# A hybrid attention and state-space decode layer on one core: one pair of state-space heads per attention head, and an output projection that opens with the attention rows of four tiles

## The chip, the cores and the metric

The kernel runs on one core of a Trainium2 chip. The metric is the device time of one execution in microseconds, lower is better. TensorE (PE) does the matmuls, VectorE (DVE) and ScalarE (ACT) the elementwise work, GpSimd (POOL) helps, and SyncE (SP) issues every DMA in one queue of instructions.

## The reference, cut to what matters

One layer mixes latent attention (8 heads) and a Mamba-2 state-space mixer (16 heads in 2 groups) over 512 prompt tokens, and takes one step for 8 decoding sequences. Both branches are gated and go through one output projection with a norm and a residual.

```python
p = softmax(q_lat @ ckv.T + q_rope @ k_rope.T)          # per attention head, causal
o_attn = (p @ ckv) @ w_uv * silu(z_attn)
y_diag = einsum('bcgls,bgjcls,bcsgjp->bclgjp', cb, exp(segsum(a)), xdt)
y_off  = einsum('bclgn,bcgjpn,bgjcl->bclgjp', cc, states, exp(a_cum))
h = exp(da)[..., None, None] * h + outer(x * dt, b)     # decode step: new state
y_s = h . c                                             # and its dot with c
g = (y + d * xs) * silu(z_ssm)
y_ssm = rmsnorm(g, per group of 512 columns)
out = x + rmsnorm(concat(o_attn, y_ssm) @ w_out)
```

## The kernel before, in words

Everything is transposed: 128 partitions hold a slice of the features, the free axis holds 512 prompt and 8 decode tokens (520 columns, worked on in two halves of 260). Each projection matmul is done as three (low part of the weights, low part of the data, high parts), so ACT rounds each weight tile of 128x1024 to `w_hi` (`hi(i)`, L553), DVE makes `w_lo` from it (`lo(i)`, L880), and then PE can use it.

The work comes in stages, each written out by hand for every engine, with semaphores between the engines and no planner:

- input projection with the paged attention of the decode tokens in its gaps, items 0 to 39 of `ITEMS` (0 to 312 us in the trace);
- states of the state-space mixer and values of attention (to about 346 us);
- the attention loop over 8 heads with the rest of the mixer in its gaps (346 to 481 us). Here one pass of the loop is called a slot: in slot s PE does the scores of head s+1 (L1758 to L1760, four blocks through three PSUM banks), the transposes of the probabilities of head s (`probs_t`, L1768), the keys of head s+2 (`keys`, L1747) and the products with the values (`outs`, L1776). DVE takes each block's maximum (`mask_max`) and the reciprocal of its sum (`inverse_sum`), ACT the exponential (`exps`, L762) and the copy of the transposes (`copy_pt`, L770), POOL scales the probabilities (`norm`), DVE gates the result (`gated`, L1224);
- the output projection (from 481.5 us), items 40 to 71: eight output tiles m for each half h, each from two weight tiles: attention rows (k2 = 0) and state-space rows (k2 = 1), eight steps k of three matmuls each. `out_square` squares the finished tile, DVE copies it out with a scale (L1352).

In the gaps of the attention loop lies the mixer:

- Eight pairs of state-space heads. A pair needs two decay tiles from ACT (`decays`, L723 and L726, each loaded by SP with `load_acb` into a ring of six), a multiplication each on DVE (`head`, L1157), PE's matmuls (`y_pair`, L1723 and L1726), and three operations on DVE that take the result out (`y_pair`, L1163 to L1165). POOL then gates it (`gate`, L1426), ACT squares it, POOL adds the squares. Before, slots 0 to 3 hold two pairs each and slots 4 to 7 none.
- After four pairs, `group_sum` totals the squares of a group on PE, `group_root` takes the root on ACT (L595), `inverse` the reciprocal on DVE (L914), `group_scale` applies it to four tiles (L1239), `ssm_high` (ACT, L780) and `ssm_low` (DVE, L1233) split each tile into the parts that the output projection reads.
- Sixteen half states of the decode step ("quads"): `state_decay` on ACT (L733), four updates on DVE (L1175) and the `dots` (L1182, L1183). Before, `SLOT_QUADS` puts ten into slots 1 to 7 and `ITEM_QUADS` six into the output projection, one to every second item. `sample_gate` and `sample_norm` follow once all are done; they release the state-space rows of the second half.

Before, the first half of the output projection starts each tile with its state-space rows; the second half starts with the attention rows. SP issues the states 2 to 7 after the last pair, then stores states 0 and 1, then loads the tiles 40 and 41, and after the last product of attention tiles 42 and 43, the residual `xres_g` and tile 44.

Of the kernel before, what the change touches and what calls it, by code (L numbers as in the profile page):

```python
# [11 lines left out]
F = mybir.dt.float32  # L12
R = mybir.dt.float32r
I32 = mybir.dt.int32
ALU = mybir.AluOpType
# [27 lines left out]
         + [("out", h, m, k, 1 - k if h == 0 else k) for h in range(2) for m in range(8) for k in range(2)])  # L43
# [7 lines left out]
NIN_UNITS = UNIT0[NIN]  # L51

# [18 lines left out]
INV0 = [0, 2, 4, 6, 7, 8]  # L71
# [7 lines left out]
for _h in range(H):  # L79
    RING += [("t", _h, 0), ("t", _h, 1)] + ([("k", _h + 2)] if _h + 2 < H else []) + [("t", _h, 2), ("t", _h, 3)]  # L80
    RING += [("sum", _h // 2 - 1)] if _h in (3, 5) else []
# [3 lines left out]
SLOT_QUADS = {1: {3: 0}, 2: {3: 1}, 3: {3: 2}, 4: {3: 3}, 5: {3: 4, 4: 5}, 6: {3: 6, 4: 7}, 7: {1: 8, 3: 9}}  # L85
ITEM_QUADS = {NIN + 2 * n: 10 + n for n in range(6)}
FIRST_NEEDS = {(NIN, 0): 13, (NIN, 6): 14, (NIN, 7): 15, (NIN + 1, 7): 16}
GROUP_SCALE = {4: (0, 1), 5: (2, 3), 6: (4, 5, 6, 7)}
SSM_HIGH = {5: (0, 1), 6: (2, 3), 7: (4, 5, 6, 7)}
SSM_LOW = {5: (0, 1), 6: (2, 3), 7: (4, 5), 8: (6, 7)}  # L90
# [16 lines left out]
def build(nc, a):  # L107
# [7 lines left out]
    def sem(name):  # L115
# [8 lines left out]
             + [at(f"hring{b}", [P, 8, NS], F, A_ + 4096 * (b - 2)) for b in range(2, NB)])  # L124
# [132 lines left out]
    a_mask = sem("mask_rounded")  # L257
# [20 lines left out]
    v_mlo, v_zs, a_zh = sem("mix_lo_done"), sem("sample_gated_copied"), sem("sample_gated_high")  # L278
# [3 lines left out]
    g_acm, g_n, g_gate, g_order = sem("acum_masked"), sem("probs_normed"), sem("ssm_gated"), sem("pool_order")  # L282
# [24 lines left out]

    def quads(s, b):

        return [SLOT_QUADS[s][b]] if b in SLOT_QUADS.get(s, ()) else []  # L310
# [29 lines left out]
    def _(sp):  # L340
        def load_item(i):
# [11 lines left out]
            elif it[0] == "qb":  # L353
                sp.dma_start(w_raw[s][:, 0:768], a["w_qb"][it[1]]).then_inc(s_wl[s], 16)
            else:
                sp.dma_start(w_raw[s], a["w_out"][it[2], it[4]]).then_inc(s_wl[s], 16)
# [120 lines left out]
        load_bcs(1)  # L477
        for t in range(5):
# [1481 lines left out]
```

## Time and profile before

| | us |
|---|---|
| median of 3 runs (592.9 to 593.53) | 593.33 |
| the profiled execution | 591.05 |
| its span | 589.3 |
| PE busy in the span | 531.9 (90%) |
| DVE busy | 384.9 (65%) |
| ACT busy | 290.6 (49%) |
| POOL busy | 77.7 (13%) |
| granted TensorE clock, mean | 0.967 |

The span is what the profiler saw; the execution is 1.75 us longer. A busy share is a mean over stages that have different limits, so the stages have to be read one by one. The clock is the share of full speed that was granted: 1.00 is the upper of its two levels (2.4 GHz), 0.50 the lower (1.2 GHz), values between are stretches with some of both.

### The profile page before, as it was taken

The numbers are of one execution on the slowest core, as the hardware profiler recorded it, in microseconds if no ns is written. First come the engines' busy times: TensorE is split into PE (matmuls) and PEld (weight loads), VectorE is DVE, ScalarE is ACT, GpSimd is POOL, SyncE is SP. The second block draws the span as 40 slices with busy tenths as digits, with TensorE's granted clock in tenths as the row PEclk, the third lists the DMA queues.
The fourth block names the chain that finished last, engine by engine and source line by source line (L and its number), as shares of the span: only waits on it lengthen the run. The fifth ranks groups of instructions, "written<-read, shape, count | busy, mean of one in ns | idle before, by whom it ended". The sixth has DMA issues, their size and how long they took to land.

```text
span 589.3 us, 12342 instructions
## 1 busy us (share of the span) xinstructions
PE 531.9 (90%) x4726; PEld 449.1 (76%) x4726; DVE 384.9 (65%) x735; ACT 290.6 (49%) x624; POOL 77.7 (13%) x102
## 2 busy tenths in 40 slices
PE   4999998999999999999998999898787639999992
PEld 4899997998888888888885456566543339999992
DVE  5674987766555677445334753767677898795675
ACT  7333232143565554552614754877858645645320
POOL 2110000000000000000002412433431000210520
PEclk9999999999999999999999999888989959999997
DMA  8233032296889877788753342432470083669552
GB/s 333 108 143 97 30 97 86 71 315 222 255 268 283 265 256 250 239 309 289 246 191 97 93 133 82 110 81 60 148 256 19 6 303 115 223 202 367 188 157 72
DMA packets 55692, 104.12 MB, mean 177 GB/s; under 512 B 7193, under 2 KB 25986, under 8 KB 55378
## 3 DMA queue, kind: packets, MB, share of 16 engines
q1 hardware_dynamic: 55634, 103.33, 53.7%
q8 instruction: 38, 0.62, 0.4%
q14 instruction: 20, 0.16, 0.1%
HBM read 95.68 MB, written 7.73 MB: 175 GB/s over the span
## 4 chain that ended last, share of the span: by engine, by line
PE 76%; DVE 14%; ACT 6%; issue 3%; DMA 1%; POOL 0%; DVEq 0%; SPq 0%; ACTq 0%
PE pm L1488 18%; PE pm L1490 16%; PE pm L1489 16%; PE px L1571 4%; PE px L1587 3%; PE px L1760 3%; PE px L1758 3%; PE pm L1709 2%; ACT dec L723 1%; PE pm L1747 1%; DVE hring L1175 1%; PE px L1700 1%; PE px L1723 1%; DVE w_lo L880 1%; DVE xbc L1239 1%
## 5 line engine op out<-in xcount | busy, mean ns | idle before, releaser
L1488 PE MATMUL pm<-xw_hi,w_lo 128*128 128x260 f32 x544 | 162.3, 298 | 9.4 <-DVE w_lo L1007 8.3
L1489 PE MATMUL pm<-xw_lo,w_hi 128*128 128x260 f32 x544 | 154.4, 284 | 0.0
L1490 PE MATMUL pm<-xw_hi,w_hi 128*128 128x260 f32 x544 | 154.2, 283 | 0.0
L1488 PEld LDWEIGHTS pm<-xw_hi,w_lo 128*128 128x128 f32 x544 | 103.0, 189 | 24.6 <-issue 11.9
L553 ACT ACTIVATE w_hi<-w_raw 128x1024 fp32r<-128x1024 f32 (+1 forms) x70 | 72.0, 1035 | 83.0 <-PE pm L1490 76.7
L880 DVE TENSOR_TENSOR w_lo<-w_raw,w_hi 128x1024 fp32r<-128x1024 f32 (+1 forms) x70 | 85.9, 1236 | 29.0 <-ACT w_hi L553 29.0
L1489 PEld LDWEIGHTS pm<-xw_lo,w_hi 128*128 128x128 f32 x544 | 103.1, 190 | 0.2
L1490 PEld LDWEIGHTS pm<-xw_hi,w_hi 128*128 128x128 f32 x544 | 103.1, 189 | 0.0
L1488 PE MATMUL pm<-mix_hi,w_lo 128*128 128x260 f32 x256 | 73.7, 288 | 11.8 <-DVE mixlo_s L1233 11.3
L1490 PE MATMUL pm<-mix_hi,w_hi 128*128 128x260 f32 x256 | 73.2, 286 | 0.0
L1488 PEld LDWEIGHTS pm<-mix_hi,w_lo 128*128 128x128 f32 x256 | 49.2, 192 | 12.4 <-issue 12.1
L1490 PEld LDWEIGHTS pm<-mix_hi,w_hi 128*128 128x128 f32 x256 | 49.0, 191 | 0.0
L1489 PE MATMUL pm<-mixlo_s,w_hi 128*128 128x260 f32 x128 | 37.0, 289 | 0.0
L1489 PE MATMUL pm<-mixlo_a,w_hi 128*128 128x260 f32 x128 | 36.1, 282 | 0.0
L1210 DVE TENSOR_REDUCE nmx<-px 128x1 f32<-128x128 f32 (+3 forms) x32 | 15.3, 484 | 25.8 <-PE px L1760 25.7
L1758 PE MATMUL px<-kn,q 128*128 128x128 f32 (+3 forms) x64 | 25.4, 481 | 7.4 <-ACT pr L762 7.3
L625 ACT ACTIVATE alpha<-nmh 128x1 f32<-128x1 f32 x32 | 9.4, 295 | 45.7 <-DVE nmh L960 45.6
L971 DVE SCALAR_TENSOR_TENSOR ckbc<-ckbc,alpha,px 128x256 f32<-128x256 f32 x32 | 15.4, 481 | 24.4 <-PE px L1587 23.8
L1420 POOL TENSOR_SCALAR pr<-pr,rsum 128x128 f32<-128x128 f32 (+3 forms) x32 | 20.4, 643 | 71.9 <-DVE rsum L1216 71.0
L619 ACT ACTIVATE ptb<-px 128x128 f32<-128x128 f32 x32 | 8.7, 273 | 42.2 <-PE px L1580 42.2
L1776 PE MATMUL pm<-pt,v 128*128 128x512 f32 (+3 forms) x64 | 22.4, 450 | 7.3 <-ACT pt L770 7.3
L947 DVE SCALAR_TENSOR_TENSOR u<-xbc,cols,u 128x511 f32<-128x511 f32 (+2 forms) x36 | 26.4, 748 | 0.8
(273 smaller groups left out, 1048.7 us busy)
## 6 DMA issues: line engine op xcount, KB each, us to landing
page<-in_cache SPq DMA_DIRECT2D x128, 288.0 KB, 3.6
w_raw<-in_w_in SPq DMA_DIRECT2D x34, 512.0 KB, 5.0
w_raw<-in_w_out SPq DMA_DIRECT2D x32, 512.0 KB, 4.7
dec<-ac_dram SPq DMA_DIRECT2D x16, 256.0 KB, 9.1
hring<-in_ssm_state SPq DMA_DIRECT2D x8, 512.0 KB, 6.5
o_ssms<-hring SPq DMA_DIRECT2D x8, 512.0 KB, 7.0
w_raw<-in_w_qb SPq DMA_DIRECT2D x6, 384.0 KB, 3.0
xraw<-in_xT SPq DMA_DIRECT2D x4, 520.0 KB, 6.4
```

What stands on the lines that cost most here:

```text
L553: act.activation(w_hi[s][:, 0:n], w_raw[s][:, 0:n], ACT.Copy).then_inc(a_whi, 1)
L880: dve.tensor_tensor(w_lo[s][:, 0:n], w_raw[s][:, 0:n], w_hi[s][:, 0:n].bitcast(F), ALU.subtract)\
L947: last = dve.scalar_tensor_tensor(b[:, s:NT], xbc[:, t, 0:NT - s], col(C_CW + 4 * t + 3 - s), b[:, s:NT], ALU.mult, ALU.add)
L1420: pool.tensor_scalar(x, x, rsum[:, k:k + 1], 0.0, ALU.mult, ALU.add).then_inc(g_n, 1)
L1488: pe.matmul(out, wl, xh, start=start, stop=False)
L1489: pe.matmul(out, wh, xl, start=False, stop=False)
L1490: return pe.matmul(out, wh, xh, start=False, stop=stop)
L1571: last = pe.matmul(px[32 * j:32 * j + 32, n % 2, lo_:lo_ + n_], w, x, start=op == 0, stop=op == 3)
L1587: last = pe.matmul(px[32 * j:32 * j + 32, 3, 0:KVR], ptb[:, n % 2, 32 * j:32 * j + 32], page[:, n % 4, j, 0:KVR], start=True, stop=True)
L1758: pe.matmul(px[:, n % 3, 0:w], q[:, h, P * b:P * b + P], kn[:, h % 2, 0:w], start=True, stop=False)
L1760: pe.matmul(px[:, n % 3, 0:w], q[:, 8 + h // 2, P * b:P * b + P], krz[h % 2][:, 0:w], start=False, stop=True)\
L1776: pe.matmul(pm[:, 3, P * kb:NT], v[:, kb, VH * h:VH * h + VH], pt[:, toff(kb):toff(kb) + NT - P * kb], start=kb == 0, stop=kb == 3).then_i ...
```

## The change

- `PAIRS`: slot 0 does two pairs of state-space heads, slots 1 to 6 one each (pair s+1). Their decays, heads, gates and squares follow the same rhythm.
- `HEAD_QUAD`: six half states in slots 1 to 6. `ITEM_QUADS`: ten in the output projection, to items 43, 44, 46, 47, 49, 50, 51, 52, 54 and 55.
- The engines' orders inside a slot are rewritten. PE puts the two first transposes before the fourth block of scores. `state_update` is taken out of `dots`.
- The group factor is made on ACT as a logarithm and an exponential (`group_log`, `group_factor`) in place of root on ACT and reciprocal on DVE. Group 0 is totalled in slot 6, group 1 after item 40.
- The output projection does, in each half, the attention rows of tiles 0 to 3, then their state-space rows, then tiles 4 to 7 one by one, attention rows first.
- The finished tile is copied out by ACT right after its square, no longer by DVE.
- SP: state 2 is loaded in the loop (it has a new place), states 0 and 1 are stored before the last pair, tiles 40 and 41 are issued right after the last pair and states 3 to 7 behind them.

```diff
-         + [("out", h, m, k, 1 - k if h == 0 else k) for h in range(2) for m in range(8) for k in range(2)])
+         + [("out", h, m, k) for h in range(2) for m0 in (0, 4, 5, 6, 7) for k in range(2)
+            for m in (range(4) if m0 == 0 else (m0,))])
+PAIRS = {0: (0, 1), **{s: (s + 1,) for s in range(1, 7)}}
+HEAD_QUAD = {s: s - 1 for s in range(1, 7)}
+ITEM_QUADS = {NIN + k: 6 + n for n, k in enumerate((3, 4, 6, 7, 9, 10, 11, 12, 14, 15))}
...
# SP, after the loads of the loop
+        load_bcs(2)
         load_ea(7)
+        store_state(0)
+        load_bcs(3)
+        store_state(1)
         sp.wait_ge(p_y, 8)
+        load_item(NIN)
+        sp.wait_ge(s_hs0, 32)
+        load_item(NIN + 1)
         for b in range(3, NB):
             load_state(b)
+        load_bcs(4)
         sp.wait_ge(s_out, 48)
         load_item(NIN + 2)
         load_item(NIN + 3)
         sp.dma_start(xres_g, a["xT"][:, 0:7]).then_inc(s_xr, 16)
...
# ACT, slot s
+            exps(s + 1, 0)
+            exps(s + 1, 1)
+            if s == 6:
+                group_log(0, r_pre)
+            copy_pt(s, 0)
+            exps(s + 1, 2)
+            if s == 6:
+                group_factor(0, r_pre)
+            copy_pt(s, 1)
+            if s:
+                mix_high(s - 1)
+                exp_ea(s + 1)
...
+            if 1 <= s <= 5:
+                decays(2 * s + 4)
+            exps(s + 1, 3)
+            if s:
+                gated_square(s)
+            if s + 2 < H:
+                copy_k(s + 2)
+            copy_pt(s, 2)
+            copy_pt(s, 3)
+            if 1 <= s <= 5:
+                decays(2 * s + 5)
+            if s + 1 in HEAD_QUAD:
+                state_decay(HEAD_QUAD[s + 1])
# ACT, output projection
         for i in range(NIN, len(ITEMS)):
             if i + 3 < len(ITEMS):
                 hi(i + 3)
+            if i == NIN:
+                group_log(1, sqs)
+                group_factor(1, sqs)
+            if i in (NIN + 1, NIN + 2):
+                for t in range(2):
+                    ssm_high(4 + 2 * (i - NIN - 1) + t)
...
# DVE, slot s
+            mask_max(s + 1, 0)
+            mask_max(s + 1, 1)
+            if 2 <= s <= 6:
+                head(2 * s + 3)
+            inverse_sum(s + 1, 0)
+            mask_max(s + 1, 2)
+            inverse_sum(s + 1, 1)
+            if n is not None:
+                state_update(n)
+            mask_max(s + 1, 3)
             if s:
                 mix_low(s - 1)
...
+            inverse_sum(s + 1, 2)
+            y_pair(PAIRS[s][0])
+            if 1 <= s <= 5:
+                head(2 * s + 4)
+            inverse_sum(s + 1, 3)
+            if n is not None:
+                dots(n)
+            if s == 6:
+                for t in range(4):
+                    group_scale(t)
             gated(s)
# DVE, between the loop and item 40
+        lo(NIN)
+        mix_low(H - 2)
+        ssm_low(0)
+        ssm_low(1)
+        gated(H - 1)
+        lo(NIN + 1)
         mix_low(H - 1)
+        ssm_low(2)
+        ssm_low(3)
# DVE, output projection
             if i + 3 < len(ITEMS):
                 lo(i + 3)
+            if i in (NIN + 2, NIN + 3):
+                ssm_low(2 * (i - NIN))
+                ssm_low(2 * (i - NIN) + 1)
+            if i in (NIN + 1, NIN + 2):
+                group_scale(2 * (i - NIN) + 2)
+                group_scale(2 * (i - NIN) + 3)
             for n in item_quads(i - 1):
+                state_update(n)
                 dots(n)
-            if i == NIN + NOUT - 4:
+            if i == NIN + NOUT + 1:
                 sample_gate()
...
# PE, slot h
             if h + 1 < H:
-                scores(h + 1)
+                scores(h + 1, range(3))
+            if h == 6:
+                group_sum(0)
             probs_t(h, 0)
             probs_t(h, 1)
-            if h < 4:
-                y_pair(2 * h)
+            if h + 1 < H:
+                scores(h + 1, (3,))
+            if h in PAIRS:
+                y_pair(PAIRS[h][0])
# PE, output projection
             for k in range(8):
-                if (i, k) in FIRST_NEEDS:
-                    pe.wait_ge(v_mlo, FIRST_NEEDS[i, k])
+                if n == 0:
+                    pe.wait_ge((v_mla, v_mls)[k2], k + 1)
...
-            if i == NIN + NOUT - 1:
+            if i == NIN:
+                group_sum(1)
+            if i == NIN + NOUT + 1:
                 pe.wait_ge(v_gs, 1)
```

## Rows read from the trace of the kernel before

**Rows 1.** Windows: busy us (and instructions) of each engine, granted clock, DMA, by slot.

```profile
core 0: us, PE busy (x) PEld busy (x) DVE busy (x) ACT busy (x) POOL busy (x), PEclk, DMA share, GB/s
366.09:384.26 18.17, 15.40 (x88) 10.82 (x87) 11.40 (x24) 14.86 (x42) 6.71 (x7) 0.88 0.44 112
384.26:403.76 19.50, 16.64 (x87) 11.86 (x87) 12.69 (x26) 15.08 (x43) 7.94 (x8) 0.85 0.32 80
...
421.44:432.00 10.56, 10.20 (x44) 6.19 (x43) 8.54 (x18) 7.89 (x19) 4.89 (x7) 1.00 0.92 318
...
448.05:462.79 14.74, 10.39 (x39) 6.03 (x38) 11.15 (x27) 11.01 (x25) 1.31 (x3) 0.88 0.07 18
462.79:481.51 18.72, 4.13 (x21) 2.33 (x19) 18.27 (x32) 8.49 (x19) 0.81 (x2) 0.75 0.46 173
481.51:500.00 18.49, 18.49 (x138) 18.49 (x139) 16.09 (x25) 11.89 (x22) 0.75 (x1) 0.88 0.49 161
```

**Rows 2.** Timeline of PE: start, length, line, operation, [idle before, releaser].

```profile
371.72 1.09 PE L1723 MATMUL px<-dec,xdt 128*64 128x128 f32 x16
...
373.51 1.88 PE L1747 MATMUL pm<-ckv,w_uk 128*128 128x512 f32 x4
...
481.51 0.56 PE L1488 MATMUL pm<-mix_hi,w_lo 128*128 128x260 f32 x1 [11.29 <-DVE mixlo_s L1233]
```

**Rows 3.** Timeline of ACT, attention loop.

```profile
376.27 1.26 ACT L723 ACTIVATE dec<-dec,acum 128x128 f32<-128x128 f32 x4
377.57 0.63 ACT L726 ACTIVATE dec<-dec 128x512 f32<-128x512 f32 x1
...
418.62 1.28 ACT L595 ACT_TABLE_LOAD   x1
```

**Rows 4.** Timeline of DVE, attention loop.

```profile
371.67 1.78 DVE L1175 SCALAR_TENSOR_TENSOR hring<-bcs,dxs,hring 128x128 f32<-128x128 f32 x4
...
378.84 0.74 DVE L1163 SCALAR_TENSOR_TENSOR xbc<-xbc,cols,px 128x512 f32<-128x512 f32 x1
...
380.69 0.68 DVE L1224 TENSOR_TENSOR u<-pm,z 128x512 f32<-128x512 f32 x1
...
430.35 3.33 DVE L914 RECIPROCAL r_pre<-r_pre 128x512 f32<-128x512 f32 x1
...
470.56 2.73 DVE L1239 SCALAR_TENSOR_TENSOR xbc<-xbc,cols,sqs 128x512 f32<-128x512 f32 x4
...
481.88 1.28 DVE L1233 TENSOR_TENSOR mixlo_s<-xbc,mix_hi 128x512 fp32r<-128x512 f32 x2
```

**Rows 5.** Timeline of POOL, slot 1.

```profile
371.23 1.28 POOL L1426 TENSOR_TENSOR xbc<-xbc,z 128x512 f32<-128x512 f32 x1
```

**Rows 6.** Timeline of ACT, output projection.

```profile
512.49 0.39 ACT L581 ACTIVATE sq<-pm 128x260 f32<-128x260 f32 x1 [0.46 <-PE pm L1490]
...
515.42 1.06 ACT L553 ACTIVATE w_hi<-w_raw 128x1024 fp32r<-128x1024 f32 x1 [0.43 <-PE pm L1490]
...
518.25 0.39 ACT L581 ACTIVATE sq<-pm 128x260 f32<-128x260 f32 x1 [1.76 <-PE pm L1490]
```

**Rows 7.** Timeline of DVE, output projection.

```profile
506.60 1.23 DVE L880 TENSOR_TENSOR w_lo<-w_raw,w_hi 128x1024 fp32r<-128x1024 f32 x1 [2.69 <-ACT w_hi L553]
...
515.85 1.13 DVE L1175 SCALAR_TENSOR_TENSOR hring<-bcs,dxs,hring 128x128 f32<-128x128 f32 x4
...
518.41 0.48 DVE L1352 TENSOR_SCALAR outp<-pm,cols 128x260 f32<-128x260 f32 x1
...
526.24 0.21 DVE L1188 TENSOR_TENSOR gs<-xbc,cols 128x64 f32<-128x64 f32 x1
...
527.46 1.21 DVE L880 TENSOR_TENSOR w_lo<-w_raw,w_hi 128x1024 fp32r<-128x1024 f32 x1
```

**Rows 8.** SP's issues of output weight tiles, and their time to landing, 468 to 475 us.

```profile
470.25 0.82 SPq L356 DMA_DIRECT2D w_raw<-in_w_out  x2
...
472.77 0.97 SPq L356 DMA_DIRECT2D w_raw<-in_w_out  x1
...
DMA to landing us min/median/max: 7.4/8.3/11.8
```

More of the change, by code:

```diff
@@ L51 @@
 NIN_UNITS = UNIT0[NIN]
+HALVES = [sum(it[0] == "out" and it[3] == 0 for it in ITEMS[:i + 1]) for i in range(len(ITEMS))]
 NSTEP = 2 * NPAGE
@@ L477, in _ @@
         load_bcs(1)
+        uk = {1: 4, 2: 5, 3: 6, 4: 7}
         for t in range(5):
@@ L802, in _ @@
         copy_k(1)
-        for s in range(-1, H):
-            h = s + 1
-            for b in range(4):
-                if h < H:
-                    exps(h, b)
-                if s >= 0 and b >= 2:
-                    copy_pt(s, b - 2)
-                if b == 1 and 1 <= s <= 4:
-                    gated_square(2 * s - 2)
-            if s < 0:
-                act.wait_ge(v_zs, 1)
-                act.activation(mix_hi[:, 0:H, NT:TT], zs, ACT.Copy).then_inc(a_zh, 1)
-                decays(5)
-                continue
+        for b in range(4):
+            exps(0, b)
@@ L845, in _ @@
+        gated_square(H - 1)
+        ssm_high(0)
+        ssm_high(1)
+        hi(NIN + 1)
         mix_high(H - 1)
+        ssm_high(2)
+        ssm_high(3)
         hi(NIN + 2)
@@ L1269, in _ @@
         dve.wait_ge(v_os, 1)
-        for s in range(-1, H):
-            h = s + 1
-            for b in range(4):
-                if h < H:
-                    mask_max(h, b)
-                if b == 0 and 2 <= s <= 3:
-                    head(4 * s)
-                    head(4 * s + 1)
-                if b == 1 and 1 <= s <= 4:
-                    y_pair(2 * s - 1)
-                for n in quads(s, b):
-                    dots(n)
-                if h < H and b:
-                    inverse_sum(h, b - 1)
-            if h < H:
-                inverse_sum(h, 3)
-            if s < 0:
-                continue
-            if s in (4, 6):
-                inverse(s // 2 + 1, (r_pre, sqs)[s // 2 - 2])
+        for b in range(4):
+            mask_max(0, b)
+            if b:
+                inverse_sum(0, b - 1)
+        inverse_sum(0, 3)
+        for s in range(H - 1):
+            n = HEAD_QUAD.get(s)
+            mask_max(s + 1, 0)
[8 more added lines that the diff above has]
+            mask_max(s + 1, 3)
             if s:
@@ L1439, in add_square @@
                 .then_inc(g_sqg, 1)
-        for s in range(-1, H):
-            h = s + 1
-            for b in range(4):
-                if h < H:
-                    norm(h, b)
-                if b == 1 and 1 <= s <= 4:
-                    gate(2 * s - 1)
-            if 1 <= s <= 4:
-                add_square(2 * s - 2)
-            if 0 <= s <= 3:
-                gate(2 * s)
-            if 1 <= s <= 4:
-                add_square(2 * s - 1)
+        for b in range(4):
+            norm(0, b)
+        for s in range(H - 1):
+            norm(s + 1, 0)
+            norm(s + 1, 1)
+            if s == 6:
+                add_square(5)
+            if s:
+                gate(s)
+            norm(s + 1, 2)
+            norm(s + 1, 3)
+            if s == 0:
+                gate(0)
+            elif s != 5:
+                add_square(s)
+        gate(H - 1)
+        add_square(H - 1)
         def out_add(h, j):
@@ L1753, in scores @@
                 pe.wait_ge(a_mask, 2)
-            for b in range(4):
+            for b in blocks:
                 n, w = 4 * h + b, P * (b + 1)
@@ L1806, in _ @@
         pe.wait_ge(v_st, 2 * NCH)
-        scores(0)
+        scores(0, range(4))
         pe.wait_ge(v_os, 1)
```

207 lines of the change are left out of this document (85 added, 122 removed).

## The prediction

> **What bounds the kernel now.** I read the slices of the page first: PE is busy nine tenths everywhere but in the attention loop and its end. The windows by slot [rows 1] size that. Slots 1 to 5 last from 366.09 to 448.05, 82.0 us, 16.4 each; slot 4, the only one with neither a pair nor a reciprocal, takes 10.56 and has PE at 10.20 busy. A pair adds 1.79 on PE (371.72 to 373.51) [rows 2], so two pairs explain 13.8 of the 18.17 and 19.50 in slots 1 and 2. The rest is waiting, and the clock: it is granted at 0.88 and 0.85 there. ACT is the fullest helper, 15.08 of 19.50, because two pairs cost it four decay tiles at 1.9 each [rows 3]. In slot 5 and slot 7 a reciprocal of 3.33 sits in DVE's queue [rows 4]. After the last product of attention PE stands still for 11.29 until 481.51 and waits for a low part that DVE makes [rows 2]; DVE is 18.27 of 18.72 busy there [rows 1]: it is behind, and it is what sets the start of the output projection. From there on PE runs solid: two items between two squares, 512.49 to 518.25, so 2.88 each [rows 6], 92.2 for the 32, and 2.2 lost to the clock at the start ((1 - 0.88) x 18.49) [rows 1].
>
> **The attention loop.** One pair per slot. PE's work in a slot is 10.20 + 1.79 = 12.0. ACT falls from 15.08 by two decay tiles to about 11.2, DVE from 12.69 by one evacuation of a pair (378.84 to 380.69, 1.85) [rows 4] and the removed reciprocals to some 10.8. Both fit under 12.0. Walking the slot in the new order, each hand-over has slack: the fourth scores need only the first exponential, made 1 us earlier; the transposes at the slot's start need POOL's last scaling, finished some 3 us before; a decay tile is loaded a slot or more before its use, and SP's new waits inside the loop (dots of quad 1, v_y of pair 5) stand in front of loads for two slots later. I take 12.1. No idle of PE means no fall of the clock either. Slots 1 to 5: 5 x 12.1 = 60.5 against 82.0, **-21.5**. Slot 0 I leave as it is.
>
> A bound from the other side: no gain, 16.4 a slot.
>
> **Slots 6 and 7.** Before, 448.05 to 470.22 (481.51 - 11.29), 22.2. Now the last pair is in slot 6, and DVE must take it out (1.85), do the dots (515.85 to 518.41 is 2.56 with the 1.13 of the updates, so 1.43) [rows 7] and four scales (2.73) [rows 4] before it gates head 6 (0.6), for which the products of head 7 wait. PE finishes the pair 9.2 into the slot (12.0 less the products); 9.2 + 6.6 + hand-overs 0.6 = 16.4, and the products of head 7, most of the 4.13 in [rows 1], end at 19.6. **-2.6**. The removed reciprocal would have been on this path. The logarithm for group 0 is in front of the second transpose: an exponential's table has to be left and fetched again.
>
> A switch of function cost ACT 1.28 in front of the root [rows 3]; I charge the same on the way to the logarithm and again to the exponential, since before has neither a logarithm nor a row that excludes either load: 0 or 1.28 each. By the Trainium skill (ScalarE: Activation LUTs, Table sets) one shipped set holds exponential and logarithm, which would make it one load in place of two. The trace agrees with the 1.28 and cannot show the rest.
>
> **From the last product to the end of the fifth item.** Before: 11.29 + 5 x 2.88 + 2.2 = 27.9. Now PE starts almost at once, on attention rows. But item 44 is the first with state-space rows, and its steps 4 to 7 need tiles 4 to 7, whose factor is made only after item 40. Let Z be the end of the last product. SP may issue item 42 only at Z (+0.4), then 43, the residual, 44. Before, 42 left at 470.25 and 44, issued at 472.77, landed 11.8 later [rows 8], 14.3 after 42. So 44 lands at Z + 14.7. Five state loads moved to just before can only make it later; I take nothing for them, as they have 10 us to drain. Then ACT and DVE go in turns, since the code puts each `hi` and `lo` before the tile work of its item: hi(44) 1.06 [rows 6], lo(44) 1.2 [rows 7], two scales 1.4, `ssm_high` 0.6, hi(45) 1.06, lo(45) 1.2, two low parts 1.3 [rows 4], two scales 1.4, `ssm_high` 0.6, hi(46) 1.06, lo(46) 1.2, two low parts 1.3, the last step 0.4: 13.8. Item 44 ends at Z + 28.5 and not at Z + 14.4. **+0.6** against before: the 11.29 of idle is not removed but moved into item 44. Its cover is only the three items 41 to 43, 8.6.
>
> **The rest of the output projection.** The same 27 items. DVE loses 16 evacuations of 0.48 [rows 7], which ACT takes at about the length of a square, 0.39, beside matmuls; it is half idle there (11.89 of 18.49) [rows 1]. At the very end the copy lies behind the square and beside PE's total, so nothing; without that cover 0.4. But DVE gets ten quads in 13 items where it had six in 11. A quad costs it 2.56, a `lo` 1.2: 3.8 in an item of 2.88. From item 43's end at Z + 28.1 it needs 14 x 1.2 + 10 x 2.56 + 1.2 for the gate (526.24 to 527.46) = 43.6, so `sample_gate` is done at Z + 71.7. PE waits for it behind item 57, which it has finished at Z + 28.5 + 13 x 2.88 = Z + 65.9. **+5.8** of standstill, where before had 0.5 at most. The weights themselves stay ahead. Both standstills are followed by half clock, 2.2 each as at 481.51: **+4.4**. The tail is the same work.
>
> **Sum.** -21.5 - 2.6 + 0.6 + 5.8 + 4.4 = -13.3. Against the profiled execution: 591.05 - 13.3 = 577.75; the median of the runs lies 2.28 above that execution, so 580.0.
>
> **Rivals.**
> - *Tiles 42 to 44 land sooner.* They had to share with the residual; with other neighbours a landing of 7.4 instead of 11.8 [rows 8] ends item 44 some 6 earlier, 574. For it: the state loads are gone from the queue by then. Against: the same three issues in the same order took what they took. Chance 0.2.
> - *The gate's wait does not bite*, because DVE regains in items 40 to 43 what I charge it later: 5.8 + 2.2 less, 572. Against: it has no gap in my walk. Chance 0.12.
> - *Fewer table loads.* Two of 1.28 leave the path, one in slot 6 and one ahead of item 44 if the load isn't what it waits for: 577.5. This is what the rule on table sets above would give. Chance 0.12.
> - *The slots don't shrink (the slower one).* Place: the hand-overs DVE, ACT, PE in slots 1 to 5. The mechanism is in the trace: four updates of a quad took 1.78 from 371.67 on, with POOL's gate running from 371.23 [rows 4, 5], and 1.13 elsewhere [rows 7]; now the updates stand in front of the fourth maximum, beside POOL's gate in every slot, and a late fourth maximum delays exponential, scaling and transposes, PE idles, and the clock falls as in slots 1 and 2. At 14.0 per slot the time is 589.5; from 14.8 the gain of 13.3 is used up; at the 16.4 of before it is 601.5. Against: some 3 us of slack in each step. Chance 0.18, of it 0.08 beyond 14.8 and 0.03 at it. The Trainium skill (GPSIMD Engine Reference, Key points) has GpSimd and VectorE share their SBUF interfaces when VectorE reads two SBUF inputs, which is this update; the trace agrees (1.78 beside POOL, 1.13 alone).
>
> **How the numbers follow.** My forecast 0.38, the rivals 0.2, 0.12, 0.12 and 0.18. A change under 0.2% can't be told from none here. Faster 0.89, same 0.03, slower 0.08. The range: down to two of the better cases together (580 - 6 - 8 = 566) and a little for slot 0, 564; up to 14.0 per slot, 589.
>
> **What would show it.** In the profile after: windows of 12 us per slot with PE near full and the clock at 1.00 (wrong: PE waiting for ACT's `pr` or `pt`, 14 and more). DVE's scales and the gate of head 6 ahead of the products of head 7. PE's largest wait inside item 44, released by `mixlo_s`, some 14 long in all, and hi(44) waiting for its load. DVE above 95% busy from item 44 to 57, then a wait of about 6 of PE on `gsum`. If the first is missing, -21.5 was wrong; if the second or third, the time is better by 6 to 14.

## The result, and the profile after

The changed kernel takes **579.9 us** (median of 4 runs, 578.05 to 581.02) against 593.43 (592.9 to 593.91) for the kernel before: a ratio of 0.9761, 95% interval 0.9733 to 0.979. It is faster by 13.5 us. The profiled execution took 580.6, with a span of 578.7.

One thing first, as every comparison below hangs on it. The input stage, which the change doesn't touch, doesn't end at the same time in every execution. The first scores of attention start here:

```profile
346.37 0.39 PE L1758 MATMUL px<-kn,q 128*128 128x128 f32 x2
...
348.97 0.39 PE L1779 MATMUL px<-kn,q 128*128 128x128 f32 x2
```

These are PE's timelines of the kernel before and of the one after. In the twelve experiments the same instruction starts at 346.47 to 346.71 seven times and at 348.85 to 348.95 five times. So I measure stages within one execution, and spans "from the scores": 242.9 before (589.3 - 346.37), 229.7 after. That is -13.2; the forecast's sum was -13.3.

The windows of the kernel after, columns as in [rows 1]: slots 0, 1 and 5 of the attention loop; slots 6 and 7 together; from the last product to the end of item 44; from there to the gate's matmul; the rest up to the last items.

```profile
353.73:367.99 14.26, 14.20 (x87) 9.15 (x86) 6.26 (x17) 8.15 (x25) 4.64 (x7) 1.00 0.44 148
367.99:379.82 11.83, 11.83 (x66) 7.61 (x65) 10.47 (x22) 8.52 (x24) 4.41 (x6) 1.00 0.71 158
...
415.31:427.14 11.83, 11.83 (x67) 7.61 (x65) 9.97 (x21) 10.45 (x31) 3.96 (x5) 1.00 0.43 126
427.14:450.79 23.65, 17.18 (x83) 10.66 (x81) 17.51 (x27) 15.19 (x35) 8.08 (x8) 0.86 0.45 166
450.79:477.80 27.01, 17.94 (x126) 16.38 (x126) 17.79 (x22) 18.30 (x29) 1.30 (x1) 0.88 0.69 239
477.80:522.95 45.15, 39.15 (x313) 38.94 (x312) 41.86 (x78) 29.50 (x62) 5.53 (x6) 0.92 0.72 220
522.95:568.30 45.35, 45.31 (x346) 44.46 (x346) 23.04 (x26) 17.67 (x30) 12.00 (x12) 0.93 0.49 146
```

The first number is the window, the second PE's busy time. In slots 1 to 5 they are equal, at full clock (slots 2 to 4 are like 1 and 5): where [rows 1] had 18.17 and 19.50, PE now never waits. From 427.14 on it does again, and the view of waits for PE names the places (line, what is awaited; total, times, longest):

```profile
PE px L1881 <- DVE gsum L1207: 6.0, 1, 6.0
PE pm L1509 <- DVE mixlo_s L1248: 5.9, 2, 3.8
PE pm L1797 <- DVE u L1239: 4.8, 1, 4.8
PE pm L1509 <- DVE mixlo_a L1243: 2.1, 1, 2.1
PE pm L1509 <- ACT sqs L592: 1.1, 1, 1.1
```

The first four are DVE's. Slots 6 and 7 (behind the wait on `u`), on DVE, POOL and PE:

```profile
430.82 3.36 DVE L1190 SCALAR_TENSOR_TENSOR hring<-bcs,dxs,hring 128x128 f32<-128x128 f32 x4
435.02 0.69 DVE L1225 TENSOR_REDUCE nmx<-px 128x1 f32<-128x512 f32 x1 [0.83 <-PE px L1781]
...
440.57 4.62 DVE L1254 SCALAR_TENSOR_TENSOR xbc<-xbc,cols,r_pre 128x512 f32<-128x512 f32 x4
445.12 0.68 DVE L1239 TENSOR_TENSOR u<-pm,z 128x512 f32<-128x512 f32 x1
```
```profile
439.23 1.19 POOL L1435 TENSOR_SCALAR pr<-pr,rsum 128x512 f32<-128x512 f32 x1 [1.31 <-DVE rsum L1231]
440.39 1.26 POOL L1453 TENSOR_TENSOR gacc<-gacc,sq 128x512 f32<-128x512 f32 x1
441.61 1.71 POOL L1441 TENSOR_TENSOR xbc<-xbc,z 128x512 f32<-128x512 f32 x1
```
```profile
445.95 2.05 PE L1797 MATMUL pm<-pt,v 128*128 128x512 f32 x2 [4.82 <-DVE u L1239]
...
450.79 0.37 PE L1509 MATMUL pm<-mix_hi,w_lo 128*128 128x260 f32 x1
```

The four scales take 4.62 where [rows 4] had 2.73; POOL is busy during 2.7 us of them. The product that then starts takes 2.05; at 436.70, ahead of the wait, the same form took 1.02. The next view has the items up to 44, with ACT and DVE in turns.

```profile
459.00 1.28 ACT L592 ACT_TABLE_LOAD   x1
460.30 0.69 ACT L592 ACTIVATE sqs<-pm,epsc 128x512 f32<-128x512 f32 x1
461.00 1.28 ACT L597 ACT_TABLE_LOAD   x1
462.30 0.63 ACT L597 ACTIVATE sqs<-sqs 128x512 f32<-128x512 f32 x1
463.50 1.06 ACT L549 ACTIVATE w_hi<-w_raw 128x1024 fp32r<-128x1024 f32 x1 [0.57 <-DMA w_raw<-in_w_out]
466.52 1.29 ACT L781 ACTIVATE mix_hi<-xbc 128x512 fp32r<-128x512 f32 x2 [1.96 <-DVE xbc L1254]
467.72 1.04 ACT L549 ACTIVATE w_hi<-w_raw 128x1024 fp32r<-128x1024 f32 x1
471.92 1.29 ACT L781 ACTIVATE mix_hi<-xbc 128x512 fp32r<-128x512 f32 x2 [3.16 <-DVE xbc L1254]
...
477.78 0.39 ACT L577 ACTIVATE sq<-pm 128x260 f32<-128x260 f32 x1 [0.33 <-PE pm L1511]
```
```profile
464.60 1.23 DVE L896 TENSOR_TENSOR w_lo<-w_raw,w_hi 128x1024 fp32r<-128x1024 f32 x1 [4.35 <-ACT w_hi L549]
465.74 1.41 DVE L1254 SCALAR_TENSOR_TENSOR xbc<-xbc,cols,sqs 128x512 f32<-128x512 f32 x2
468.79 1.23 DVE L896 TENSOR_TENSOR w_lo<-w_raw,w_hi 128x1024 fp32r<-128x1024 f32 x1 [1.65 <-ACT w_hi L549]
469.94 1.29 DVE L1248 TENSOR_TENSOR mixlo_s<-xbc,mix_hi 128x512 fp32r<-128x512 f32 x2
...
475.33 1.28 DVE L1248 TENSOR_TENSOR mixlo_s<-xbc,mix_hi 128x512 fp32r<-128x512 f32 x2
```

Each engine is idle while the other works: 4.35 and 1.65 on DVE, 1.96 and 3.16 on ACT. The logarithm has a load ahead of it and the exponential another, 1.28 each.

### The profile page after: what moved, and what is told of

Its sections match the earlier page's. It is cut to its first block, busy times and chain, and to the rows that moved or that the text cites. A ratio compares the mean times of both kernels' runs of the same rounds, so it can differ in the third digit from the quotient of the medians.

```text
span 578.7 us, 12372 instructions
## 1 busy us (share of the span) xinstructions
PE 531.7 (92%) x4726; PEld 450.4 (78%) x4726; DVE 379.3 (66%) x717; ACT 297.3 (51%) x642; POOL 78.9 (14%) x102
## 4 chain that ended last, share of the span: by engine, by line
PE 75%; DVE 14%; ACT 4%; issue 3%; DMA 3%; SPq 0%; DVEq 0%; ACTq 0%
PE pm L1509 16%; PE pm L1511 14%; PE pm L1510 14%; PE px L1592 4%; PE pm L1797 3%; PE px L1608 3%; PE px L1781 3%; DVE w_lo L896 3%; PE px L1779 3%; PE pm L1768 2%; PE pm L1730 2%; DMA w_raw<-in_w_out 2%; DVE hring L1190 2%; ACT w_hi L549 2%; PE pm L1789 1%
## 5 line engine op out<-in xcount | busy, mean ns | idle before, releaser
L1509 PEld LDWEIGHTS pm<-xw_hi,w_lo 128*128 128x128 f32 x544 | 103.5, 190 | 24.7 <-issue 11.9
L896 DVE TENSOR_TENSOR w_lo<-w_raw,w_hi 128x1024 fp32r<-128x1024 f32 (+1 forms) x70 | 85.2, 1220 | 44.4 <-ACT w_hi L549 44.3
L1509 PE MATMUL pm<-mix_hi,w_lo 128*128 128x260 f32 x256 | 76.0, 297 | 9.1 <-DVE mixlo_s L1248 5.9
L1511 PE MATMUL pm<-mix_hi,w_hi 128*128 128x260 f32 x256 | 74.6, 291 | 0.0
L1509 PEld LDWEIGHTS pm<-mix_hi,w_lo 128*128 128x128 f32 x256 | 50.7, 198 | 10.4 <-DVE mixlo_s L1248 6.6
L1511 PEld LDWEIGHTS pm<-mix_hi,w_hi 128*128 128x128 f32 x256 | 50.6, 198 | 0.0
L1797 PE MATMUL pm<-pt,v 128*128 128x512 f32 (+3 forms) x64 | 24.4, 482 | 4.8 <-DVE u L1239 4.8
L1190 DVE SCALAR_TENSOR_TENSOR hring<-bcs,dxs,hring 128x128 f32<-128x128 f32 x64 | 27.8, 494 | 0.0
L1425 POOL TENSOR_TENSOR xdte<-xdt,toend 128x512 f32<-128x512 f32 x8 | 10.2, 1278 | 121.2 <-DVE xdt L1152 121.2
```

Source lines behind the costliest of these rows:

```text
L896: dve.tensor_tensor(w_lo[s][:, 0:n], w_raw[s][:, 0:n], w_hi[s][:, 0:n].bitcast(F), ALU.subtract)\
L1190: dve.scalar_tensor_tensor(hring[b][:, t, :], bcs[b % 2][:, g, :], dxs[:, 0, t, b:b + 1], hring[b][:, t, :], ALU.mult, ALU.add).then_inc(v ...
L1509: pe.matmul(out, wl, xh, start=start, stop=False)
L1511: return pe.matmul(out, wh, xh, start=False, stop=stop)
L1797: pe.matmul(pm[:, 3, P * kb:NT], v[:, kb, VH * h:VH * h + VH], pt[:, toff(kb):toff(kb) + NT - P * kb], start=kb == 0, stop=kb == 3).then_i ...
```

## The experiments

Each is the changed kernel with the edit shown. "From the scores" is the span of the profiled execution less the start of the first scores in it; it comes from one execution, the median from four (six in experiment 9). The two measures differ by up to about 4 us in what they make of an edit, so both are given.

| | experiment | us (range) | ratio to before | from the scores |
|---|---|---|---|---|
| | kernel after | 579.9 (578.05 to 581.02) | 0.9761 | 229.7 |
| 1 | head 6's gate first | 574.02 (573.29 to 575.45) | 0.9693 | 226.5 |
| 2 | item 44's tiles at once | 573.66 (570.17 to 574.45) | 0.967 | 223.3 |
| 3 | 1 and 2 | 568.43 (566.26 to 571.01) | 0.9573 | 217.9 |
| 4 | 2, opens with two tiles | 575.21 (573.78 to 577.37) | 0.9697 | 225.3 |
| 5 | residual later | 576.19 (575.96 to 576.36) | 0.9731 | 227.6 |
| 6 | root and reciprocal | 584.62 (584.0 to 586.94) | 0.9885 | 233.5 |
| 7 | thin half states, loop | 577.07 (576.22 to 578.65) | 0.9725 | 227.7 |
| | thin half states, projection | 571.19 (568.9 to 572.78) | 0.9626 | 220.4 |
| 8 | 3, half states early | 569.82 (569.41 to 571.46) | 0.9592 | 223.1 |
| 9 | 8, residual later, head 7 first | 569.69 (569.28 to 574.33) | 0.9614 | 221.1 |
| 10 | 9, gate's matmul later | 570.35 (569.35 to 572.45) | 0.9612 | 219.3 |
| 11 | 10, one half state ahead of item 40 | 566.09 (565.18 to 569.81) | 0.9544 | 216.2 |

My theory: three walls stand behind the loop, all DVE's: `u` ahead of the last products, the rows of item 44, the gate's sums. The rivals, one for each: the fourth maximum late through the state update; the landing of item 44's weights; a stall that PE would have wherever it asks.

**1. Head 6's gate ahead of the four scales.**

```
+            gated(s)
             if s == 6:
                 for t in range(4):
                     group_scale(t)
-            gated(s)
```

> The changed kernel (579.9) with one move: in slot 6 DVE gates head 6 before the four scales of group 0. Theory: PE's wait of 4.82 before the products of head 7 is DVE's order and nothing else. The products then start about 4.6 earlier, at full clock (2.7 for them in place of 4.84), and the scales fall into time in which DVE waited (3.76) for ACT's high parts. The end of the last product comes 5 to 7 earlier, but item 44 hangs on item 42's issue at that end, so it comes earlier too: total 573 to 575. Rival: the scales are then late for the low parts and for item 40's last step, and the gain is lost in items 40 to 44: total 578 to 580.

574.02. From the start of slot 6 (424.64) to the first matmul of the output projection is 445.02 - 424.64 = 20.38 instead of 23.65, and the wait on `u` is gone: the last product ends at 442.04, 17.4 into the slot. A new one stands one place on: the scales now delay the low part of item 40's weights. PE:

```profile
445.02 0.59 PE L1509 MATMUL pm<-mix_hi,w_lo 128*128 128x260 f32 x1 [2.98 <-DVE w_lo L896]
```

So 3.3 us are won up to there, and all of the gain is made there (3.2 from the scores): a wait of 4.8 was cured, and one of 3.0 took its place.

**2. The rows of item 44 in one piece.** The four scales, then the four low parts, ahead of the next weight tile's low part; the four high parts together on ACT.

```
+            if i == NIN + 1:
+                for t in range(4, 8):
+                    group_scale(t)
+                for t in range(4, 8):
+                    ssm_low(t)
             if i + 3 < len(ITEMS):
                 lo(i + 3)
-            if i in (NIN + 2, NIN + 3):
...
```

> The changed kernel with one reordering: the four scales, high parts and low parts of tiles 4 to 7 are done in one go, before hi(44) on ACT and lo(44) on DVE, and not in turns with hi and lo of items 44 to 46. Theory: item 44 is late because of the turns. The last low part is ready some 7 earlier, PE's two waits on mixlo_s (2.11 and 3.77) vanish and with them most of the half clock after: item 44 ends 18 to 21 after the last product in place of 26.9, total 571 to 574, if DVE's gate wait of 6.0 behind item 57 stays as it is. Rival one, the loads decide: hi(44) waited for its load anyway, so item 44 ends at most 2 earlier, total 578. Rival two, DVE decides: what item 44 gains comes back as a longer wait behind item 57 (12 in place of 6), total 579.

573.66. The waits on `mixlo_s` are gone; what stays inside item 44 is 2.1 on `w_lo`. From the last product (450.76) to item 44's square is 22.0 instead of 27.0, and the item behind it takes 2.88 instead of 4.58, as PE doesn't come out of a standstill at half clock. The sums' wait is 6.4.

**3. Both.**

> The first two edits together: head 6 of the attention before the gate of the last slot, and item 44's ssm tiles first. By the spans from the start of the attention loop they saved 3.2 and 6.4 us alone. Theory (one cures the wait behind slot 6, the other the wait before item 44, two places): most of both is kept, 7 to 9 us from 579.9, so 571 to 573 us. Rival (both are paid for by the same VectorE backlog that the gate's sums wait for): the wait on gsum grows to 8 to 9 us and 573.5 to 575 us result, no better than the second alone.

568.43, below what I expected. By medians the two saved 5.9 and 6.2 and together 11.5; from the scores 3.2 and 6.4 and together 11.9, which is 2.3 more than the sum, and no run here shows why. They add at least, and the rival of one common backlog falls. The two largest waits of PE in this kernel:

```profile
PE px L1879 <- DVE gsum L1206: 6.4, 1, 6.4
PE pm L1507 <- DVE w_lo L895: 5.1, 2, 3.0
```

**4. Opening with two tiles.** Experiment 2, with the first half of the projection opening on the attention rows of two tiles.

```
+         + [("out", h, m, k) for h in range(2) for m0 in ((0, 2) if h == 0 else (0,)) + (4, 5, 6, 7) for k in range(2)
+            for m in (range(m0, m0 + 4 - 2 * (h == 0)) if m0 < 4 else (m0,))])
```

> The kernel with the pair of ssm tiles of item 44 first, and the first half of the output projection opens with the attention rows of two tiles (as the second item list of the kernel before did with its halves) instead of four; so the Mamba rows are asked for after four items instead of eight. Theory (the four-tile opening is what gives the chain of the Mamba rows time: some 12 us of PE work in four items more): PE meets item 42 with the first state rows about 11 us earlier, of which the rows' chain can't follow; waits on the mixed rows grow by 3 to 5 us, and 577 to 579 us result against 573.7. Rival (DVE's total work until the gate's sums is the bound, and the order of the items only places the wait): the wait on gsum shrinks by what the new waits take, and 573 to 575 us result.

575.21, between the two: 1.6 slower by medians, 2.0 from the scores. PE waits 4.20 on `mixlo_s` instead of 2.1 on `w_lo`, and the sums' wait stays at 6.4. The ranges of the two kernels overlap, but the wait agrees with the difference. So the four-tile opening is worth about 2 us with the rows' chain already shortened; how much it gave with the chain of the changed kernel was not run.

**5. The residual's load four items later.**

```
-        sp.dma_start(xres_g, a["xT"][:, 0:7]).then_inc(s_xr, 16)
...
+            if i == NIN + 8:
+                sp.dma_start(xres_g, a["xT"][:, 0:7]).then_inc(s_xr, 16)
```

> The changed kernel with the residual (1820 KB) issued behind item 47's tile in place of ahead of item 44's. Rival of the prediction (tiles land sooner): item 44's load is what the chain begins with, so item 44 ends 5 to 6 earlier and the total is 574. Theory after the trace: ACT waited only 1.40 for item 43's load and 0.57 for item 44's; between them lie two table loads, logarithm and exponential. So the chain can start at most 2.0 earlier: total 578 to 579.9.

576.19, 3.7 less by medians and 2.1 from the scores, against 0 to 1.9 expected and 5.9 by the rival. Item 44 ends 25.95 after the last product instead of 27.0, and `mixlo_s` is waited for 5.6 instead of 5.9. So the landing is worth 1 us. A further 0.9 is the item behind it at 3.72 instead of 4.58; that varies: 4.76 in experiment 1, 3.53 in experiment 7, after waits of the same 3.8 to 4.2.

**6. Root on ACT and reciprocal on DVE in place of logarithm and exponential.**

```
-            act.activation(dst[:, 0:NT], pm[:, bank(("sum", g)), :], ACT.Ln, bias=epsc, scale=1.0 / NORM_WIDTH[3 + g])\
+            act.activation(dst[:, 0:NT], pm[:, bank(("sum", g)), :], ACT.Sqrt, bias=epsc, scale=1.0 / NORM_WIDTH[3 + g])\
...
+                dve.reciprocal(r[:, 0:NT], r[:, 0:NT]).then_inc(a_gf, 1)
```

> The changed kernel with one part undone: the group factors are made by a root on ACT and a reciprocal on DVE as before, in place of logarithm and exponential on ACT. Theory: DVE gets 3.3 twice, in slot 6 in front of the scales that delay the gate of head 6, and in front of the scales of tiles 4 and 5; ACT loses 0.6 twice and one table load before item 44 (the one back to the exponential). Slot 6: 2.5 to 3.3 later. Item 44: 3.3 less 1.9, 1.4 later. Total 583 to 585. Rival: the reciprocal lies in time in which DVE waits, total 580.

584.62: the logarithm form is worth 4.7 by medians and 3.8 from the scores. DVE between the dots and the gate of head 6:

```profile
440.28 3.34 DVE L1252 RECIPROCAL r_pre<-r_pre 128x512 f32<-128x512 f32 x1
...
443.66 2.74 DVE L1255 SCALAR_TENSOR_TENSOR xbc<-xbc,cols,r_pre 128x512 f32<-128x512 f32 x4
```

The wait on `u` is 6.31, only 1.5 more for a reciprocal of 3.34, because the same four scales, now begun when POOL's gates of this place are over, take 2.74 and not 4.62. The total lies in the forecast range, but not by the parts that were forecast: the start of the output projection is 0.9 later in its slot (expected 2.5 to 3.3), and from there to item 44's square it takes 30.0 instead of 27.0 (expected 1.4 more), with 8.4 of waiting on `mixlo_s` instead of 5.9.

**7. Thin half states.** Two kernels whose state updates and dots work on 16 of 128 state columns (so they leave out 112 columns of the new state and of its output): one in the six half states of slots 1 to 6, one in the ten of the projection.

```
+            c = 16 if n < 6 else NS
...
+                dve.scalar_tensor_tensor(hring[b][:, t, 0:c], bcs[b % 2][:, g, 0:c], dxs[:, 0, t, b:b + 1], hring[b][:, t, 0:c], ALU.mult, ALU.add).then_inc(v_h, 1)
```

> The changed kernel with less work on DVE in the attention loop: the six half states of slots 1 to 6 are updated and dotted in 16 of their 128 state columns only (112 are left out). Theory: slots 1 to 5 are bound by PE, so they stay at 11.83 each to the hundredth, although DVE loses about 2 of its 10 in each. In slot 6 DVE's queue sets the gate of head 6: the dots (1.4) shrink to about 0.4, so PE's wait of 4.82 falls by about 1, total 1 to 2 less, 578 to 579. Rival: the slots hang on DVE and shrink by 0.3 or more each, total 576 or less.

> The changed kernel with less work on DVE in the output projection: the ten half states there are updated and dotted in 16 of 128 state columns only (112 are left out). Theory: DVE saves about 1.9 in each of ten, the sample's gate is ready long before item 57 ends, PE's wait of 6.0 on gsum vanishes with the half clock behind it (2.2), total 571 to 572. Item 44 ends where it did. Rival: the wait is released by something else (the weights of item 60, the load for item 58 for which ACT waited 2.2), then 3 or more of the 6.0 stay: total 575 to 577.

In the loop (577.07, between the 578 expected at least and the rival's 576) they are free: from the scores to slot 6 is 78.16 against 78.17. In slot 6 the update shrinks from 3.36 to 0.80, and the maximum behind it doesn't move, 432.71 - 424.83 = 7.88 into the slot as in the kernel after (435.02 - 427.14):

```profile
428.52 0.80 DVE L1191 SCALAR_TENSOR_TENSOR hring<-bcs,dxs,hring 128x16 f32<-128x16 f32 x4
432.71 0.69 DVE L1227 TENSOR_REDUCE nmx<-px 128x1 f32<-128x512 f32 x1 [3.39 <-PE px L1783]
```

What this kernel still gains lies in the dots ahead of `u` (last product 23.0 into slot 6 instead of 23.65) and in the clock behind item 44. The wait on `u` falls only from 4.8 to 4.6 and not by 1: `u` is ready 0.7 earlier in the slot, and PE asks for it 0.5 earlier. In the projection the same edit gains 8.7 (9.3 from the scores): the sums' wait falls from 6.0 to 0.8, though item 44 waits no less (6.8 on `mixlo_s`, before 5.9). This leaves the work out and moves it nowhere. The window from item 44 to the gate:

```profile
474.90:513.91 39.01, 38.21 (x312) 38.00 (x311) 27.42 (x78) 29.52 (x62) 4.51 (x6) 0.98 0.75 241
```

**8. The ten half states one or two items earlier,** on experiment 3, with the rows of their `bcs` buffer loaded four items earlier.

```
-ITEM_QUADS = {NIN + k: 6 + n for n, k in enumerate((3, 4, 6, 7, 9, 10, 11, 12, 14, 15))}
+ITEM_QUADS = {NIN + k: 6 + n for n, k in enumerate((1, 2, 4, 5, 7, 8, 10, 11, 13, 14))}
...
-        bc_after = {NIN + 13: 5, NIN + 16: 6, NIN + 19: 7}
+        bc_after = {NIN + 9: 5, NIN + 12: 6, NIN + 15: 7}
```

> The changed kernel with the gate of head 6 first, the state-space tiles 4 to 7 in one go, and the ten half states of the output projection moved ahead, to items 41, 42, 44, 45, 47, 48, 50, 51, 53 and 54 (the loads of their rows three to four items earlier). The first two edits gave 5.9 and 6.2 less by themselves; if they add, 568. Theory on the quads: two in three items are 2 x 3.7 + 1.1 = 8.5 of DVE in 8.64 of PE, so DVE keeps up, the last is done at item 55 and the wait on gsum falls from 6.0 to under 1, with the half clock 6 to 8 less: total 560 to 562. Rival: the two early ones delay lo(45) and lo(46) and PE waits there instead, 4 or more: total 564 to 567.

A miss: 569.82, no better than experiment 3 and 5.2 worse from the scores. The wait on the sums was to fall under 1 and is 5.4, and the waits on `w_lo` are 7.2 instead of 5.1. The edit moved a wait into SP's queue. SP after the last product:

```profile
471.99 2.90 SPq L354 DMA_DIRECT2D w_raw<-in_w_out  x3
481.10 0.38 SPq L429 DMA_DIRECT2D bcs<-bc_dram  x1
481.52 0.73 SPq L354 DMA_DIRECT2D w_raw<-in_w_out  x1
```

The load of `bcs` waits for the dots that still use its buffer, from 474.89 to 481.10, and no weight tile goes out in that time. ACT's waits of that stretch, first in this kernel and then in experiment 3:

```profile
ACT w_hi L549 <- DMA w_raw<-in_w_out: 12.2, 5, 4.0
...
ACT w_hi L549 <- DMA w_raw<-in_w_out: 0.7, 1, 0.7
```

DVE then idles 4.4 of 49.9 us (45.51 busy) where it idles 1.6 of 46.1 in experiment 3. So the queue accounts for DVE's idle time, and with it for the wait on the sums that stays; no run takes that wait out of the queue, so this is argued from the trace. It doesn't account for all of the 5.2: 1.1 comes earlier, where ACT waits 2.3 for the tiles of items 42 and 43 and not 1.2, loads that the edit doesn't touch; 2.7 lies between there and the sums, 1.4 behind them. The profiled execution was also the slowest of its four (571.46, the others 569.41 to 570.06).

**9. On 8, the residual later and head 7's rows first.**

```
         lo(NIN)
         mix_low(H - 2)
-        ssm_low(0)
-        ssm_low(1)
         gated(H - 1)
-        lo(NIN + 1)
         mix_low(H - 1)
+        lo(NIN + 1)
+        ssm_low(0)
+        ssm_low(1)
```

> The kernel of the run before it in this list, with two more edits: the residual issued behind item 47's tile, and between the loop and item 40 the gate and low part of head 7 ahead of the low parts of tiles 0 and 1 (ACT likewise makes head 7's high part first). Theory: PE's wait of 2.1 for head 7's low part in item 40 falls to under 1, and item 42's and 44's loads come up to 1.4 earlier: 2 to 3 less, 558 to 560. Rival: item 40 then waits for its own weights, whose low part DVE makes behind the scales, and nothing changes.

That is DVE's order; ACT makes its high parts in the same one. 569.69, the same by medians, 2.0 less from the scores; the sums' wait is 5.6. The wait for head 7's low part, which the edit was to shorten, stood in the kernel after (2.1) but isn't in experiment 8 at all: the gate of head 6 ahead of the scales had already removed it. That reordering had nothing to win.

**10 and 11. The gate's matmul two items on; then one half state ahead of item 40.**

```
-            if i == NIN + NOUT + 1:
+            if i == NIN + NOUT + 3:
                 pe.wait_ge(v_gs, 1)
...
# 11, and no half state at item 41
         ssm_low(2)
         ssm_low(3)
+        state_update(6)
+        dots(6)
```

> The combination of the last run (quads early, residual later, head 7 first) and, besides, the column sums' matmul two items further back on PE (behind item 59 instead of 57), the gate's norm behind item 60 instead of 59, the inverse one item later. Theory (the 6.0 us wait is VectorE's total work between item 41 and item 57, met by PE wherever it asks for the sums): PE goes on with items 58 and 59, about 5.8 us of work, while VectorE finishes; the wait on gsum falls from 5.6 to 0 to 1 us, and 566 to 568 us result against 569.7, less than the whole 5.6 because the norm's chain behind the sums is then met at item 61 or 62 with some 2 to 3 us. Rival (the rest of the gate's chain is as long as the wait): the wait only moves to the first matmul that needs the norm, 569 to 570 us.

> As the kernel with the sums' matmul behind item 59, and one of the output projection's ten half states (a 128 x 512 scale row and its dots, some 2.5 us of VectorE) is done before item 40, in time in which VectorE waits for ScalarE. Theory (VectorE's total work from there to item 57 is the bound): 1 to 2.5 us less than that kernel, 564.5 to 567 us. Rival (this half state delays the w_lo of items 40 to 42, which PE waits for): the waits on w_lo grow by 2 to 3 us and nothing is won, or it is 1 us slower.

In 10 the steps behind the matmul (root, norm, inverse) come one or two items later too. Experiment 10: 570.35, no gain that its median shows, 1.8 from the scores. By its total the rival is nearer than the theory. PE goes through items 58 and 59 at full clock, and the sums aren't waited for. The wait is then met by the matmul that needs the rows made from them; PE in 10:

```profile
515.54 0.29 PE L1880 MATMUL px<-gsum,cm 128*128 128x16 f32 x2
...
518.57 0.36 PE L1508 MATMUL pm<-mix_hi,w_lo 128*128 128x260 f32 x1 [2.73 <-DVE mixlo_s L1219]
```

2.73 for 5.62. Half of what was left of the gain went into waits on `w_lo` (6.7 to 8.1). Experiment 11: 566.09, 4.3 less by medians, 3.1 from the scores. The half state fills idle time of DVE ahead of item 40; PE's waits on `w_lo` grow by only 0.5, and ACT still waits 16.4 for weight tiles. Of the 3.1, 2.0 lies ahead of the sums' matmul and can be put down to the moved half state. The other 1.2 lies behind it, and there the clock differs:

```profile
518.57:530.00 11.43, 11.43 (x79) 11.31 (x80) 4.88 (x5) 4.57 (x8) 0.67 (x1) 0.85 0.69 264
...
516.90:530.00 13.10, 13.08 (x106) 12.98 (x107) 8.03 (x8) 4.26 (x8) 3.70 (x4) 1.00 0.61 234
```

These windows begin right behind the wait for the rows, which was 2.73 in experiment 10 (first line, clock 0.85) and 3.16 in experiment 11 (second line, clock 1.00). Nothing in the edit accounts for that.

Experiment 11 is the fastest kernel here, 0.9544 (0.9485 to 0.9602), below both kernels; against experiment 3 (0.9516 to 0.9629) the intervals overlap. Experiment 3 with the last two edits but with SP's old order wasn't run.

## Why the prediction was right, point by point

- **Slots 1 to 5, -21.5:** right. They last 5 x 11.83 = 59.15 against 81.96, -22.8. The term is 0.17 a slot under the 12.1 that was taken. The rival that slots don't shrink had its ingredient: the update beside POOL takes 2.3 in slots 1 to 5 and 3.36 in slot 6 [rows 4 had 1.78, rows 7 1.13]. But the slack argued for was there. Thin, the update lets DVE idle 1.25 in front of the fourth maximum of slots 1 to 5, and the maximum comes only 0.2 earlier in the slot; the slots don't change (experiment 7). No run puts the pairs back two to a slot, so how the 22.8 divides between the pairs, the new orders inside the slot and the reciprocals that left it is open.
- **Slots 6 and 7, -2.6:** this is the term that was mis-sized. They take 23.65 against 22.17, **+1.5**. The order of events was as written: PE finishes the pair, DVE takes it out, dots, scales, gate, then the products. I had PE start the products 16.4 into slot 6 and end them at 19.6; they started at 445.95 - 427.14 = 18.8 and ended at 23.65. Of the 2.4, 1.9 is the scales (4.62 instead of 2.73). The other 0.5 is the pair: PE finished it 9.7 into the slot and not 9.2, behind a wait of 1.1 for ACT's logarithm, which the walk didn't have. A further 1.6 is the products, 4.84 where 3.2 was charged: they ran at half clock after the 4.82 of waiting (at full clock they took 3.0, experiment 1), a price that I had charged to the other two standstills and not to this one. The sentence "four scales (2.73)" took a row measured with POOL idle for a place with POOL at work, although the argument about the updates had just that effect in it.
- **Table loads:** the charge of 1.28 ahead of the logarithm and again ahead of the exponential was right: four loads stand in the trace, at 430.56, 433.05, 459.00 and 461.00. The rival of fewer loads falls: one set for both functions, as the prediction considers it, was not what this program loaded.
- **Last product to item 44, +0.6:** measured -0.9 (27.0 against 27.9). The chain of turns began 12.7 after the last product and not 14.7, and then took 0.5 longer. Waits of 2.1 (`mixlo_a`) and 1.1 came earlier than the walk had them, and the turns of ACT and DVE are as written (hi, lo, scales, highs) from 463.50 on: 14.3 to the square against 13.8. hi(44) waited for its load, but the residual's part in that is 1 us (experiment 5), so the rival that priced an earlier landing at 6 was mis-priced as well: the logarithm, the exponential and their two loads kept ACT until 462.93 anyway. The turns are the cost (experiment 2).
- **The gate, +5.8:** measured 6.0, against 0.5 before. "From item 43's end at Z + 28.1" names the wrong event: 28.1 is where the walk has DVE finish the low parts for item 44; the sum from there is as it should be. The step rested on DVE's work from item 44 to item 57, and experiment 7 shows it: thin, the wait is 0.8. It hardly depends on what goes before (6.0 in experiments 1, 5 and 6, 6.4 in 2 and 3), which fits that a later start of item 44 is later for both engines. So the rival "DVE regains it in items 40 to 43" didn't come true. "Above 95% busy" was too much: 41.86 of 45.15, 93%; 1.7 of the idle 3.3 is a wait on ACT's `w_hi`.
- **Half clock, +4.4:** from item 44 to the last square the time grew by 9.7 (477.78 to 567.31, against 79.8 before) where gate and clock were to make it 10.2. The two prices can be read apart. The item behind item 44 took 4.58 instead of 2.88, 1.7 more. From the sums' matmul to the last square took 44.4, and 41.6 at clock 1.00 with thin half states (experiment 7), 2.7 more. Together 4.4, as charged, though split 1.7 and 2.7 and not 2.2 twice. The stage grew by less than 10.2 mostly because the kernel before had 0.5 of waiting of its own there.
- **The sum:** -22.8 + 1.5 - 0.9 + 9.7, with -0.7 ahead of slot 1 and nothing at the tail, gives the -13.2 read directly. Against the forecast the terms are off by -1.3, +4.1, -1.5 and -0.5, and by -0.7 where nothing was charged. They cancel, and that is luck: the place, the waits and their owners were forecast, but 580.0 against 579.9 is far closer than the terms deserve.

## What to carry to other kernels

When a stage is rebalanced until the matmul engine is solid in it, look for the next place where a helper's total work between two fixed points exceeds the matmul engine's: moving the point at which the result is asked for won a third of a wait of 5.6 (1.8, experiment 10), leaving most of the helper's work out won nearly all of it (9.3 with the clock, experiment 7), and moving one of ten pieces of work out of the stretch won about 2 (experiment 11). Take a duration for a moved instruction from a row with the same neighbours on the other engines, and charge the half clock at each standstill as long as those that rows show it behind, not at the largest ones alone. A load that waits for a buffer stalls every load behind it on its queue, so moving compute earlier pays only if the queue's order can follow.

## What was not expected of the hardware

- **DVE beside POOL.** The same four 128 x 512 scales took 4.62 us where two of POOL's two-input operations ran beside them (kernel after), 5.14 where there were three (experiment 3), and 2.74 with POOL quiet (experiment 6, same place). The four 128 x 128 updates took 3.36 in slot 6 beside three operations of POOL, 1.13 alone. Lines of DVE and POOL in experiment 3:

```profile
430.80 3.36 DVE L1189 SCALAR_TENSOR_TENSOR hring<-bcs,dxs,hring 128x128 f32<-128x128 f32 x4
441.15 5.14 DVE L1253 SCALAR_TENSOR_TENSOR xbc<-xbc,cols,r_pre 128x512 f32<-128x512 f32 x4
```
```profile
431.45 1.29 POOL L1451 TENSOR_TENSOR gacc<-sq,sq 128x512 f32<-128x512 f32 x1
432.70 1.32 POOL L1439 TENSOR_TENSOR xbc<-xbc,z 128x512 f32<-128x512 f32 x1
441.60 1.73 POOL L1439 TENSOR_TENSOR xbc<-xbc,z 128x512 f32<-128x512 f32 x1
444.48 1.27 POOL L1451 TENSOR_TENSOR gacc<-gacc,sq 128x512 f32<-128x512 f32 x1 [1.15 <-ACT sq L566]
```

  POOL pays too: its gate took 1.71 and 1.73 there against 1.27 in experiment 6, where a reciprocal of DVE ran beside it, and that one kept its 3.34 [rows 4]. The slowing is shown for these places; what the two engines share is not shown by these runs. The Trainium skill (GPSIMD Engine Reference, Key points) has GpSimd share its SBUF interfaces with VectorE and contend with VectorE instructions that have two SBUF inputs. The runs agree: the slowed scales and updates read two tiles of SBUF, and the reciprocal that kept its 3.34 beside the same gate reads one.
- **The end of the unchanged input stage** falls into two groups: the scores start at 346.37 to 346.71 or at 348.85 to 348.97. The shift is there already where the input projection ends (310.85 before, 313.46 after). Nothing was run to find out why, and a difference of 2 us between two single executions means nothing until it is taken away.
- **The price of half clock behind the same wait** ranged from 0.65 to 1.9 us (the item behind item 44 at 3.53 to 4.76, against 2.88 at full clock, after waits of 3.8 to 4.2). Whether it is paid varies too: a wait of 2.73 was followed by a granted clock of 0.85 in experiment 10, one of 3.16 by 1.00 in experiment 11.
